# Differential attention: one unrolled sequence of units, and the product with the values as one f32 matmul

## The reference, cut to what matters

```python
s = einsum('...qhcd,...khcd->...hcqk', q, k) * ATTN_SCALE
s = where(mask, s, -inf)                   # chunk-causal: 64 rows see whole chunks of 64
p = softmax(s, axis=-1)
w = p[..., 0, :, :] - lam * p[..., 1, :, :]
o = einsum('...hqk,...khe->...qhe', w, v)
return rms_norm(o, subln_g) * (1.0 - lam_init)
```

## Time and profile before

| | |
|---|---|
| runs of before | 3261.34, 3262.35, 3263.57 us; median 3262.35 |
| profiled execution | its span, first to last instruction, 3257.2 us; the page gives no other time for this execution; the median of the runs is 5.15 us above this span |
| PE busy | 2812.7 us, 86% of the span |
| mean granted TensorE clock | 0.928 of full speed (2.4 GHz; 0.50 is 1.2 GHz) |
| projection ends, windowed attention ends | about 548 and 832 us |
| first matmul, first scores, last computation of differential attention | 845.0, 893.7, 1546.0 us |

### The profile page before, as it was taken

How to read it: one execution, slowest core, us unless ns; L and a number is a source line. 1 busy time by engine, 2 the same in 40 slices (tenths; PEclk the granted TensorE clock), 3 DMA queues, 4 the chain that set the end, 5 groups by cost and what they waited for, 6 DMA issues and landing times. The chain is left out here.

```text
span 3257.2 us, 59293 instructions
## 1 busy us (share of the span) xinstructions
PE 2812.7 (86%) x20248; PEld 1715.0 (53%) x20248; DVE 1685.5 (52%) x3210; ACT 1236.9 (38%) x2288; POOL 330.1 (10%) x481
## 2 busy tenths in 40 slices
PE   0999994677477788887599799999999999999998
PEld 0666662444244555665255456556565565565654
DVE  6555552676788898655555241432423414424336
ACT  2344443566186777887344211111121111111213
POOL 0112222000311223323000000000000000000001
PEclk9999997676589899997799899999999999999999
DMA  4344442111401000110322201101001011010002
GB/s 166 120 171 167 156 165 92 32 48 40 92 13 27 20 5 8 35 31 11 123 77 71 71 0 39 39 0 39 12 26 39 0 39 39 0 39 18 20 13 106
DMA packets 136130, 179.99 MB, mean 55 GB/s; under 512 B 60304, under 2 KB 99184, under 8 KB 134928
## 3 DMA queue, kind: packets, MB, share of 16 engines
q1 hardware_dynamic: 136016, 178.53, 16.9%
HBM read 133.92 MB, written 42.17 MB: 54 GB/s over the span
## 5 line engine op out<-in xcount | busy, mean ns | idle before, releaser
L1960 ACT ACTIVATE silu<-gate_ps,scales 128x352 f32<-128x352 f32 x132 | 73.2, 554 | 1140.2 <-PE up_ps L2000 1140.2
L1891 DVE SCALAR_TENSOR_TENSOR act<-up_ps,scales,silu 128x352 f32<-128x352 f32 x132 | 77.1, 584 | 778.2 <-ACT silu L1960 778.2
L1998 PE MATMUL gate_ps<-ffn_inT_hi,gate_hi 128*128 x1056 | 330.8, 313 | 15.1 <-DVE up_lo L1879 15.1
L1903 DVE SCALAR_TENSOR_TENSOR residual_rows<-down_ps,scales,residual_rows 128x512 f32<-128x512 f32 (+1 forms) x374 | 278.8, 748 | 118.4 <-PE down_ps L2010 117.4
L1999 PE MATMUL gate_ps<-ffn_inT_lo,gate_hi 128*128 x1056 | 330.7, 313 | 0.0
L2000 PE MATMUL gate_ps<-ffn_inT_hi,gate_lo 128*128 x1056 | 330.6, 313 | 0.0
L2000 PE MATMUL up_ps<-ffn_inT_hi,up_lo 128*128 x1056 | 330.0, 313 | 0.0
L1998 PE MATMUL up_ps<-ffn_inT_hi,up_hi 128*128 x1056 | 330.0, 313 | 0.0
L1999 PE MATMUL up_ps<-ffn_inT_lo,up_hi 128*128 x1056 | 330.0, 313 | 0.0
L2008 PE MATMUL down_ps<-down_hi,act_hi 128*128 128x512 f16 (+1 forms) x748 | 283.8, 379 | 0.0
L2009 PE MATMUL down_ps<-down_lo,act_hi 128*128 128x512 f16 (+1 forms) x748 | 283.5, 379 | 0.0
(11 more groups left out here) (296 smaller groups left out, 6143.3 us busy)
## 6 DMA issues: line engine op xcount, KB each, us to landing
w_scan<-in_w_gate SPq DMA_DIRECT2D x16, 704.0 KB, 6.4
w_scan<-in_w_up SPq DMA_DIRECT2D x16, 704.0 KB, 7.7
w_scan<-in_w_down SPq DMA_DIRECT2D x16, 704.0 KB, 4.0
gate<-in_w_gate SPq DMA_DIRECT2D x22, 512.0 KB, 5.9
up<-in_w_up SPq DMA_DIRECT2D x22, 512.0 KB, 7.4
down<-in_w_down SPq DMA_DIRECT2D x22, 512.0 KB, 3.6
keys_values<-in_w_in SPq DMA_DIRECT2D x8, 1152.0 KB, 15.7
x_tile<-in_x SPq DMA_DIRECT2D x17, 512.0 KB, 3.5
```

Source lines behind the costliest of these rows:

```text
L1903: nc.vector.scalar_tensor_tensor(H[0:rows, at:at + 512], YP[(2 * t + n) % 4][0:rows, :], SC[0:rows, S_YI:S_YI + 1], H[0:rows, at:at + 512] ...
L1998: nc.tensor.matmul(out, FH[w][:, k, c], nh, start=k == 0, stop=False)
```

## The change

In the projection the values are written once, in f32, by ACT (tile V32, in the place of VH and VL); DVE's low half of the values goes. POOL fills only the column of ones.

In differential attention:

- All units of all heads form one list of 352, written out without loops. The cached stage comes first. The diagonal units change shape: instead of four of 4, 3, 2, 1 blocks there is one with the four diagonal blocks and two full ones of 4 and 2 blocks, so the counts of blocks and of score columns stay.
- Values: one f32 matmul of 129 columns for each block, f32 weights (the probabilities) by f32 values, three units behind (`LAG`) the scores. PH, PL, the second exp, the casts and the subtractions go. There are 5 f32 tiles for full units and 2 each for the others.
- Maxima are spread over the sequence by a planner that gives each piece a cost and each head a due time (6 units ahead); pieces for up to 8 heads run ahead. `maxima`, the transposes and the copy to Q2 (two tiles) are made per head: 20 times instead of 5, just ahead of the head.
- SP loads the cached stage's queries first, copies the keys in three parts (cached, first four tiles, rest), and fills K2's two extra rows by DMA from a small tile. POOL's fills go; DVE clears a quarter of the two diagonal tiles.
- Squares move from ACT to POOL, their sum to DVE (`square_sum`); POOL keeps a power and the scaling. The w_out scan takes whole rows and stays in the last stage.

```diff
@@ phase_project, DVE
-    nc.vector.scalar_tensor_tensor(KN[:, :, HD:P], ..., ALU.mult, ALU.subtract)
-    nc.vector.scalar_tensor_tensor(vtile(VL, i)[:, :, 0:VD],
-                                   vs.rearrange("p (h e) -> p h e", e=VD), col(S_A),
-                                   vtile(VH, i)[:, :, 0:VD], ALU.mult, ALU.subtract).then_inc(kv_lo, 1)
+    nc.vector.scalar_tensor_tensor(KN[:, :, HD:P], ..., ALU.mult, ALU.subtract).then_inc(kv_lo, 1)
@@ phase_project, ACT
-    nc.scalar.activation(vtile(VH, i)[:, :, 0:VD], vs.rearrange("p (h e) -> p h e", e=VD),
+    nc.scalar.activation(vtile(V32, i)[:, :, 0:VD], vs.rearrange("p (h e) -> p h e", e=VD),
                          ACT.Copy, scale=col(S_A)).then_inc(kv_hi, 1)
@@ build
-            VH, VL = KV[:, nk:nk + nv], KV[:, nk + nv:nk + 2 * nv]
+            V32 = KV[:, nk:nk + 2 * nv].bitcast(f32)
@@ the units
+LAG = 3
+RING = 5
+AHEAD = 8
...
+    if gr.frame:
+        yield "meta", [(TS, 0, 0, 4)], slice(DEC, DEC + META), ((slice(DEC, DEC + META), slice(0, P)),), 4 * P
+        for t in range(t0):
+            yield "full", [(t, 0, 0, 4)], every, ((every, slice(0, P)),), 4 * P
+        yield "diag", [(t0 + j, j * P, j, 1) for j in range(4)], every, ((every, slice(CH, P)), (slice(0, CH), slice(0, CH))), 4 * P
+        yield "full", [(t0, 0, 1, 3), (t0 + 2, 3 * P, 3, 1)], every, ((every, slice(0, P)),), 4 * P
+        yield "full", [(t0 + 1, 0, 2, 2)], every, ((every, slice(0, P)),), 2 * P
@@ SP
+                load_q1(0)
+                load_ql(0)
+                copy_keys(0, NT, NKT)
+                sp.wait_ge(mrow_ok, 1)
+                sp.dma_start(K2[HD:HD + 2, :, :]..., CM[:, :].unsqueeze(1).broadcast_to([2, HC * NKT, P])).then_inc(k2_in[0], 16)
+                load_q1(1)
+                load_ql(1)
+                copy_keys(1, 0, 4)
+                copy_keys(2, 4, NT)
@@ POOL
+                def squares(gr):
...
+                    nc.gpsimd.tensor_tensor(SQ[:, 0:gr.nq, :], v, v, ALU.mult).then_inc(sq_ok, 1)
+                def scale(gr):
...
+                    nc.gpsimd.tensor_tensor(RS[x][:, 2, q], RS[x][:, 1, q], CO[:, 4:4 + gr.nq], ALU.pow).then_inc(rs_ok, 1)
...
+                    nc.gpsimd.tensor_tensor(OD[x][:, q, :], OD[x][:, q, :],
+                                            RS[x][:, 2, q].unsqueeze(2).broadcast_to([P, gr.nq, VD]), ALU.mult).then_inc(f_ok, 1)
@@ DVE
+                for k in range(END):
+                    for p in plan.at[k] if k < K else ():
+                        reduce_piece(p)
+                    nxt = plan.starts(k + 6)
+                    if nxt is not None:
+                        maxima(groups[nxt])
+                    if k in ratio_at:
+                        ratio(*ratio_at[k])
+                    if k in square_sum_at:
+                        square_sum(square_sum_at[k])
+                    if k in scan_at:
+                        scan_w_out(scan_at[k])
@@ ACT
+                def exps(u):
+                    act.wait_ge(s_ok, u.k + 1)
+                    if plan.prev[u.k] is not None:
+                        act.wait_ge(av_ok, plan.prev[u.k] + 1)
+                    for rows, n in u.parts:
+                        view = lambda T: T[rows, 0:u.cols].rearrange("p (j n) -> p j n", n=P)[:, :, n]
+                        last = nc.scalar.activation(view(PF[u.buf]), view(SP[u.k % 2]), ACT.Exp,
+                                                    scale=SC[rows, S_SC:S_SC + 1])
+                    last.then_inc(e_ok, 1)
+                for k in range(K):
+                    exps(units[k])
+                    nxt = plan.starts(k + 3)
+                    if nxt is not None:
+                        q2T_out(groups[nxt])
@@ PE
+                def scores(u):
+                    if u.k > 1:
+                        pe.wait_ge(e_ok, u.k - 1)
...
+                def values(u):
+                    pe.wait_ge(e_ok, u.k + 1)
...
+                    for t, at, q0, n in u.blocks:
+                        for q in range(q0, q0 + n):
+                            out = OP[u.c][:, q // 2, (q % 2) * VW:(q % 2 + 1) * VW]
+                            last = nc.tensor.matmul(out, PF[u.buf][r, at + (q - q0) * P:at + (q - q0 + 1) * P], vt(V32, t, gr.h, r),
+                                                    start=first and q % 2 == 0, stop=u.k == plan.last[gr.index, u.c],
+                                                    skip_group_check=True)
+                    last.then_inc(av_ok, 1)
...
+                for k in range(K + LAG):
+                    if k + 2 < K:
+                        scores(units[k + 2])
+                    for p in plan.at[k] if k < K else ():
...
+                        max_piece(p)
+                    nxt = plan.starts(k + 4)
+                    if nxt is not None:
+                        q2T(groups[nxt])
+                    if k >= LAG:
+                        values(units[k - LAG])
```

More of the change, by code:

```diff
@@ L1077, in phase_differential @@
+def phase_differential(g, K1, V32):
+    nc, dram = g.nc, g.dram
+    plan = DiffPlan()
+    units, groups, K = plan.units, plan.groups, plan.K
     with ExitStack() as ctx:
         K2 = g.sb("kT_hi_max", [HD + 2, HC, NKT * P], f16, ctx)
-        QL = g.sb("dq_lo_max", [P, 4, HC, HD + 2], f16, ctx)
-        Q1 = [g.sb(f"dqT_hi_hi{n}", [P, HC, 4 * P], f16, ctx) for n in range(3)]
-        Q2 = g.sb("dqT_lo_max", [HD + 2, HC, 4 * P], f16, ctx)
-        widths = {"meta": 4 * P, "cached": P, "new": P}
@@ L1083, in phase_differential @@
[L1083 to L1088 removed]
+        CM = g.sb("max_row_const", [2, P], f16, ctx)
@@ new lines, in phase_differential @@
+        QL = [g.sb(f"dq_lo_max{n}", [P, 4, HC, HD + 2], f16, ctx) for n in range(2)]
+        Q1 = [g.sb(f"dqT_hi_hi{n}", [P, HC, 4 * P], f16, ctx) for n in range(2)]
+        Q2 = [g.sb(f"dqT_lo_max{n}", [HD + 2, 2, 4 * P], f16, ctx) for n in range(2)]
+        sizes = {("full", n): 4 * P for n in range(RING)}
+        sizes |= {(kind, n): 4 * P for kind in ("meta", "diag") for n in range(2)}
+        sizes |= {(kind, n): P for kind in ("cached", "new") for n in range(2)}
+        PF = {b: g.sb(f"dp_{b[0]}{b[1]}", [P, w], f32, ctx) for b, w in sizes.items()}
@@ L1089, in phase_differential @@
+        MP_ = g.sb("drow_max_parts", [P, AHEAD, 4, 2, NPIECE_SLOTS], f32, ctx)
+        MX = [g.sb(f"drow_max{n}", [P, 4, 2], f32, ctx) for n in range(2)]
         RD = g.sb("dden", [P, 3, 4], f32, ctx)
@@ new lines, in phase_differential @@
+        n_stages = len(plan.stage_first) - 1
+        q_loads = lambda stage: 16 * sum(groups[4 * x].nq for x in range(stage + 1) if (x - stage) % 2 == 0)
+        scan_at = {plan.first[4 * (n_stages - 1) + m // 2] + 16 + 8 * (m % 2): m for m in range(KC)}
+        ratio_at = {plan.last[gr.index, c] + LAG + 1: (gr, c) for gr in groups for c in range(2)}
+        square_sum_at = {plan.last[gr.index, 1] + LAG + 3: gr for gr in groups}
+        scale_at = {plan.last[gr.index, 1] + LAG + 5: gr for gr in groups}
@@ L1221, in _ @@
+                for k in range(END):
+                    if k in ratio_at and ratio_at[k][1] == 1:
+                        squares(ratio_at[k][0])
+                    if k in scale_at:
+                        scale(scale_at[k])
             @block.vector
             def _(dve):
[L1224 to L1227 removed]
@@ L1487, with bank_free, max_piece @@
-NORM_LAG = 2
-SCAN_STAGE = 3
-SCAN_AT = (5, 7, 9, 11)
-SQUARE_LAG = 4
-def pieces_after(st, nxt, u):
-    return range(u * nxt.NP // st.U, (u + 1) * nxt.NP // st.U) if nxt else ()
-def sq_base(st):
-    return 3 * HDIF * st.n
+                def bank_free(before):
+                    if before is not None:
+                        kind, n = before
+                        pe.wait_ge(red_ok if kind == "piece" else q2_out, n + 1)
+                def max_piece(p):
+                    bank_free(p.before)
+                    hc = 2 * p.g.h + p.c
+                    for q, at, key, w in p.runs:
+                        last = nc.tensor.matmul(MB[p.bank][:, at:at + w], Q1[p.g.stage % 2][:, hc, q * P:(q + 1) * P],
+                                                K1[:, hc, key:key + w], start=True, stop=True)
+                    last.then_inc(mx_ok, 1)
```

706 lines of the change are left out of this document (304 added, 402 removed).

## The result

The changed kernel takes 3090.96 us (median of 4 runs, 3086.72 to 3094.75) against 3261.85 us: a ratio of 0.9477, 95% interval 0.9464 to 0.9491, 171 us less. The profiled execution's span is 3085.4 us. Forecast were 3100 us and a range of 3045 to 3245. The four runs lie in two pairs, 3086.7 and 3087.2, 3094.7 and 3094.8, and the profiled one is of the lower pair, so a difference of some 4 us between two kernels' medians says nothing.

The account below looks back on a forecast made before the run. PE, 86% busy, was taken to wait in turn for ACT and DVE, no single bound. First scores at 853, 519 us plus 10 allowance, end 1389 against 1546.0: -157, with projection -160; 3262.35 became 3102, said 3100 us, range 3045 to 3245.

Parts of the forecast that it names:

- The f32 product, the term that decides: Values product in differential attention: four passes with loads hidden, 230 ns a block against 172, +72 us of PE work.
- Rival E: Values product: one f32 matmul takes one pass, 57.5 ns a block; DVE and the start bind, about 2950 us; chance 0.02.
- rival C: Values product: weight loads half hidden, one of 107 ns showing per block, 337 ns; 3234 us; chance 0.07.
- Rival D: Values product: f32 weight loads become the bound, four of 107 ns, 428 ns a block; slower, 3347 us; chance 0.15.
- Rival F: Differential attention: f32 work leaves the clock at 0.50, PE's 490 us double; about 3590 us; chance 0.03.
- ACT and DVE: Differential attention: second exp, low halves and casts go; ACT falls from 503 to about 250 us, DVE from 542 to some 320.
- The added lag of three units covers what is left: Values product behind scores: waits for exp (29.6 us) go, and the longer lag covers any remainder.
- The start: Start of differential attention: first scores at 853 us, between 846 and 865, instead of 893.7; -41 us.
- The projection: End of the projection: one low-half pass fewer in the chain of four tiles PE waits for; -3 us.
- The cached stage: Cached stage of differential attention: kept at 31 us, as a chain of latencies with one exp less and 17 pieces more.
- The frame stages: Frame stages 0 to 3: PE's work 55 (raised from 45 for DVE), 95, 145 and 186 us, plus transposes 7.
- rival B: Differential attention: PE newly waits for reductions and maxima through the shared maximum banks; 3152 to about 3180 us; chance 0.10.

Follow-up runs that it names:

- e9: Changed kernel with value matmuls of all short units (meta, cached, new) run over all 128 rows, padded with zeros: 3062.73 us, ratio 0.9396.
- e12: Changed kernel with only the cached stage's short units (cached, new) over all 128 rows, meta units keeping 16: 3072.97 us, ratio 0.942.
- e5: Changed kernel with the small copy of K2's two extra rows issued first in the queue: 3094.09 us, ratio 0.9467; two of six runs 3075.0 and 3075.8.
- e4: Changed kernel with the values product one unit behind the scores instead of three: 3092.23 us, ratio 0.9485.
- e8: Changed kernel with one f16 matmul a block in place of the f32 one, low halves left out: 2917.12 us, ratio 0.8944.

## Why the prediction was right, point by point

**The f32 product, the term that decides: right.** 222.5 ns a block for 230, four times 55.6. That is the time of four f16 passes with the loads hidden, as taken; it makes the term 1248 x (222.5 - 172) = 63 us instead of 72. The rule of the Trainium skill (FP8 and Floating Point Precision, TensorE Precision Notes) that true FP32 takes four passes agrees with these 222.5 ns. Rival E (one pass) falls by the spacing, rival C (one load shown, 337 ns) too.

**Rival D, the f32 load as the bound: half right in its ground, wrong in its result.** The records do show a longer load, 193 ns. But two of them stand behind a block, not four, and they overlap: 222.5 ns lies far under the 360 from which it would have decided. The Trainium skill (TensorE: Matmul & The Clock Gate, LDWEIGHTS (loading the stationary operand)) has 107 ns for a load of 128 columns, from which the estimate of 3347 us came: 428 ns a block if each of four passes loads by itself and in turn. The trace has 222.5, so the measurement decides against that reading.

**Rival F, the half clock: wrong for f32 as such, not for all of it.** The frame stages had 1.00 over 482 us of mostly f32 work. The cached stage had 0.50. Over 128 rows the same f32 work had 1.00 (e9, e12), so there it was not f32 that held it either; the split of e5's runs leaves open whether the 16 and 64 rows did.

**ACT and DVE: right in kind, DVE's relief undersized.** 241 us for 250 and 283 for 320 in the phase; in the whole kernel 263 and 271 us less, where 250 and 220 had been named as signs. (ACT's four terms as written add up to 228, not to 250.)

**"The added lag of three units covers what is left": wrong.** The waits for exp went, from 29.6 to 0.2 us, but they went as well with a lag of one (e4). The sentence ahead of it had the reason: the exp (0.69 us) is shorter than its unit on PE.

**The start: the mechanism right, the size under.** First scores at 845.5, and at 847.8 without the projection's 2.3 us, which the sum counts apart, for 853 (846 to 865); the queries came earlier than put, and what was late was the small row copy, 5.6 us, which putting it first in the queue does not save (e5).

**The projection: right.** The chain's last transposes start at 539.02 instead of 541.32, 2.3 us for 3.

**The cached stage: mis-sized.** "For the cached stage I keep 31 us": it took 40. I read 31 us from the earlier trace rows as a chain of latencies. Now PE had no gap in it, and the term was to be made from PE's sum: 41,122 columns pass, the f32 ones counted twice, at 0.43 ns some 18 us, and at the half clock, where matmuls of 128 columns start 107 ns apart, 34; the other 7 are lost where the row count changes (e9), a cost that the forecast did not have. It was luck that the miss of ten microseconds did no harm: the allowance of 10, made for refills and the clock, was not needed for refills and covered it.

**The frame stages: right in the sum.** 55 + 95 + 145 + 186 + 7 = 488 for 481 (49.6, 98.7, 148.2 and 184.4 with their transposes). The raise of stage 0 for DVE was not needed, a block was 7.5 ns cheaper than put, and 8.5 us at the meta units (e9) that nobody had priced went the other way. No refill between heads shows, and rival B's new wait didn't come (nothing for a reduction or a maximum in the list of waits, after the first), since DVE had half the time to spare.

**Slips that decide nothing.** By the chances as written the range leaves out 0.22, not 0.20. PE's work with one pass a block comes to 278 us by the prediction's own prices, not 310; e8, which is that case, took 2917 us for rival E's 2950.

**What the prediction did not ask** is whether the two parts of the change need each other. Its statement on frame stage 0, "nobody is the bound, each waits for each", is the likely reason why both pay alone, 72 and 188 us, and why they don't add: each cures in part the same waits. A sum for PE with the sequence and the f16 halves, 72 us lower than the forecast's, beside DVE's and ACT's, near full, would have shown that variant as the nearer rival.

## What to carry to other kernels

When a change has two parts that both answer the same wait, work out the time with each part alone from the engines' sums: here the f32 product was worth 72 us in an order where ACT and DVE held PE up, and cost 18 us in one where they did so less. A block in f32 cost PE 222.5 ns and three f16 matmuls 171, and the trade was good only where the engines that make the halves were late. Look at the granted clock beside "PE busy": the cached stage was full for 40.7 us and had some 18 us of work at 1.00 in it, and "full" is the records' latency: compare the distances between their starts. Mixed row counts are a thing to remove. And look at the single runs, not only at their median, before a variant is called no different (e5).

## What was not expected of the hardware

- **One f32 matmul is two records**, 111 ns each for 129 columns at clock 1.00, each with a weight load of about 190 ns; those loads overlap one another and hide, at 222.5 ns a block.
- **Going between matmuls of 16 and of 128 rows cost PE some 0.1 us at clock 1.00**, and not the small matmul itself; between 66 and 128 rows nothing shows: the 16-row units lost 0.28 us each in f32 and 0.19 in f16, at their borders. Padding with zeros to 128 rows took 8.5 us from the frame stages.
- **The clock stayed at 0.50 through some 35 us without a gap of PE in the profile**, and came to 1.00 within 10 us of the first scores when the same value matmuls ran over 128 rows, on the same data. The row count is not all of it: the kernel before ran its short units over 128 rows and had 0.50 in its cached stage as well, where PE was busy 24 of 31 us. With a lag of one the clock was up for 14 us in that stage and down again, and two of e5's six runs were 20 us shorter than the others with the same code. What decides is open.
